# Four small edits to a hybrid attention decode kernel: two weight loads and eight gate halves moved, eight semaphores joined into one, five extra matmuls

## What is computed

```python
def _project_in(x, pos, norm_pre, w_in, ...):
    xn = _rmsnorm(x, norm_pre)
    (qa, kvc, kvs, kvw, gn, ga, qd, kvd, krp, gb, ma, mb) = jnp.split(xn @ w_in, IN_OFFSETS, axis=-1)
...
def _mla_attend(q_lat, q_pe, t, c, kr, pos_k):
    s = (jnp.einsum('bqhc,bsc->bhqs', q_lat, c) + jnp.einsum('bqhr,bsr->bhqs', q_pe, kr)) * MLA_SCALE
    mask = (pos_k[None, :] <= t[:, None])[None, None]
    p = _masked_softmax(s, mask)
    return jnp.einsum('bhqs,bsc->bqhc', p.astype(c.dtype), c)
...
def _merge_out(x, o_a, o_lat, gates, ...):
    pa = (o_a * jax.nn.silu(ga)) @ w_proj_a
    pb = (o_b * jax.nn.silu(gb)) @ w_proj_b
    h = jax.nn.sigmoid(ma) * pa + jax.nn.sigmoid(mb) * pb
    return x + _rmsnorm(h @ w_out, norm_post)
```

## Time and profile before

| | us |
|---|---|
| median of 3 runs | 703.12 |
| all runs | 701.88, 703.12, 706.72 |
| the profiled execution | 701.88 |
| its span, first to last instruction | 700.1 |
| outside of the span | 1.8 |
| PE busy in the span | 666.3 (95%) |
| mean granted clock of TensorE | 0.996 of full |

### The profile page before, as it was taken

One profiled execution on the slowest core, in us unless ns is written; L12 is line 12 of the kernel. 1 busy time (PEld: TensorE's weight loads), 2 busy tenths in 40 slices (PEclk: granted clock), 3 DMA queues, 4 the chain that ended last, 5 costly groups with the idle time before them and its releaser, 6 DMA issues.

```text
span 700.1 us, 15279 instructions
## 1 busy us (share of the span) xinstructions
PE 666.3 (95%) x5767; PEld 439.9 (63%) x5767; DVE 437.8 (63%) x1231; ACT 211.5 (30%) x579; POOL 63.9 (9%) x68
## 2 busy tenths in 40 slices
PE   9999999999999978899999998799999999999996
PEld 4444444644476655667677686578778888885452
DVE  3297899688677757766566565427486656553344
ACT  0402214565344444434444433211101111110211
POOL 0353441031000000220211000000000000000000
PEclk9999999999999999999999999999999999999999
DMA  8999996888899999978858889965411111045010
GB/s 338 414 415 418 419 418 279 308 252 285 315 311 384 386 400 388 401 248 287 304 166 305 310 268 360 391 259 203 158 60 61 61 60 61 1 163 229 30 61 32
DMA packets 66371, 178.65 MB, mean 255 GB/s; under 512 B 7065, under 2 KB 15538, under 8 KB 59258
## 3 DMA queue, kind: packets, MB, share of 16 engines
q1 hardware_dynamic: 55672, 124.88, 49.0%
q0 software_dynamic: 7840, 48.38, 17.3%
q10 hardware_dynamic: 2786, 4.42, 1.8%
HBM read 169.12 MB, written 12.72 MB: 260 GB/s over the span
## 4 chain that ended last, share of the span: by engine, by line
PE 80%; DMA 8%; DVE 5%; SPq 3%; ACT 2%; issue 2%; DVEq 0%; ACTq 0%
PE bank L1420 19%; PE bank L854 12%; PE bank L1460 8%; PE bank L1264 7%; DMA ring<-latent 4%; PE bank L1131 4%; PE bank L1233 4%; PE bank L1248 4%; PE bank L1153 3%; PE bank L1017 3%; PE bank L1139 3%; DMA projP<-x 3%; PE bank L1452 2%; SPq L627 2%; PE bank L1200 2%
## 5 line engine op out<-in xcount | busy, mean ns | idle before, releaser
L854 PE MATMUL bank<-W,XG 128*128 128x494 f32 x192 | 83.6, 580 | 0.9 <-DVE projP L1793 0.9
L2447 DVE TENSOR_TENSOR projP<-projP,bank 128x260 f32<-128x260 f32 x83 | 33.8, 422 | 45.2 <-PE bank L1420 44.4
L1264 PE MATMUL bank<-W 128*128 128x260 f32 x256 | 60.4, 389 | 0.0
L1678 ACT ACTIVATE projP<-bank,projP 128x128 f32<-128x128 f32 (+3 forms) x96 | 49.7, 524 | 30.9 <-DVE projP L2149 30.5
L1481 ACT ACTIVATE projP<-bank 128x128 f32<-128x128 f32 (+5 forms) x87 | 33.9, 391 | 83.0 <-PE bank L1420 47.5
L854 PEld LDWEIGHTS bank<-W,XG 128*128 128x128 f32 x192 | 35.2, 192 | 36.6 <-issue 35.0
L1481 ACT ACTIVATE W<-bank 128x512 f32<-128x512 f32 (+2 forms) x69 | 40.1, 582 | 55.2 <-PE bank L897 13.3
L1264 PEld LDWEIGHTS bank<-W 128*128 128x128 f32 x256 | 47.4, 190 | 11.0 <-issue 4.1
L2149 DVE CUSTOM_DVE_ANT_0 bank<-bank,maskb 128x128 f32<-128x128 f32 (+3 forms) x96 | 45.6, 509 | 7.8 <-PE bank L1131 7.1
L1460 PE MATMUL bank<-ring,W 128*128 128x512 f32 x112 | 49.6, 594 | 0.0
L1131 PE MATMUL bank<-W 64*128 64x128 f32 (+7 forms) x192 | 46.1, 467 | 1.1 <-ACT projP L1678 0.7
(11 more groups left out here) (434 smaller groups left out, 1109.8 us busy)
## 6 DMA issues: line engine op xcount, KB each, us to landing
ring<-latent SPq DMA_DIRECT2D x200, 256.0 KB, 5.1
XG<-latent SPq DMA_DIRECT2D x56, 256.0 KB, 5.4
W<-w_gate SPq DMA_DIRECT2D x12, 1024.0 KB, 6.2
W<-w_attn SPq DMA_DIRECT2D x16, 494.0 KB, 12.4
rope_rows<-ring SPq DMA_DIRECT2D x8, 512.0 KB, 7.3
KRR<-rope_rows ACTq DMA_DIRECT2D x16, 256.0 KB, 5.9
ring<-w_out SPq DMA_DIRECT2D x2, 2048.0 KB, 9.5
o_win<-win SPq DMA_DIRECT2D x1, 4088.0 KB
```

Of the source, the lines that this page charges most:

```text
L854: mm = pe.matmul(bank[2 * (u % 2) + n][:, 0:GW], XG[:, k * TOK + tl * P:k * TOK + (tl + 1) * P], w_part(half, k, n), start=(k == 0), stop= ...
L1264: mm = pe.matmul(bank[6][:, 0:HALF], gate_w[g % 2][:, at:at + P], X2[:, k * TOK + hf * HALF:k * TOK + (hf + 1) * HALF], start=(k == 0), st ...
L1678: act.activation(Pb[u % 4][:, 0:w], bank[u % 2][:, 0:w], ACT.Exp, bias=NMp[:, u:u + 1], scale=-1.0, accum_out=RSp[:, u:u + 1]).then_inc(S[ ...
```

## The change

Four edits:

1. `G_at`: half 6 goes from step 33 to 31, 7 from 34 to 33, 8 from 37 to 34, 9 from 38 to 35, 10 from 41 to 37, 11 from 43 to 38, 12 from 45 to 41, 13 from 47 to 43. Steps 31 and 35 gain a half, steps 45 and 47 lose theirs. The apply steps follow.
2. The second halves of `w_attn` all signal one semaphore, `w_in_rest`, and PE waits once, ahead of unit 4, until all eight have landed.
3. On SP gate(3) goes from behind part 23 to behind part 21, gate(4) from behind part 29 to behind part 24.
4. Ahead of the wait for the latent part of pairs 6, 12, 13, 14 and 15, PE runs one more matmul of 128x512 into bank 5, whose result nobody reads.

```diff
-        G_at = {d: i for i, d in enumerate((23, 25, 26, 27, 29, 30, 33, 34, 37, 38, 41, 43, 45, 47, 48, 49))}
+        G_at = {d: i for i, d in enumerate((23, 25, 26, 27, 29, 30, 31, 33, 34, 35, 37, 38, 41, 43, 48, 49))}
...
             for k in range(KM):
-                sp.dma_start(W[:, (KM + k) * 2 * GW:(KM + k + 1) * 2 * GW], t["w_attn"][:, k, 2 * GW:]).then_inc(S[f"w_in{k}"], 16)
+                sp.dma_start(W[:, (KM + k) * 2 * GW:(KM + k + 1) * 2 * GW], t["w_attn"][:, k, 2 * GW:]).then_inc(S["w_in_rest"], 16)
...
             gate(2)
-            for m in range(19, 24):
+            for m in range(19, 22):
                 latents(m)
             gate(3)
-            for m in range(24, 30):
+            for m in range(22, 25):
                 latents(m)
             gate(4)
+            for m in range(25, 30):
+                latents(m)
...
                 for k in range(KM):
-                    if u == 4:
-                        pe.wait_ge(S[f"w_in{k}"], 32)
+                    if u == 4 and k == 0:
+                        pe.wait_ge(S["w_in_rest"], 16 * KM)
...
                     pe.wait_ge(S["dp"], mla[p2]["q"])
+                if i2 == 0 and p2 in KEPT_BUSY:
+                    pe.matmul(bank[5][:, :], ident, qrT[:, 0:512], start=True, stop=True)
                 job_landed(pe, J_MLA + m)
...
+            KEPT_BUSY = (6, 12, 13, 14, 15)
```

## The result

The change took 711.19 us in the median of 8 runs (708.47 to 713.39), the kernel before 705.90 in the median of 8 (701.88 to 707.75). The ratio is 1.0084 with an interval of 1.0054 to 1.0113: slower by 5.9 us, worked out on 705.9 (the medians differ by 5.3). The profiled execution took 711.43 us, its span is 709.6.

A forecast was written before the change was run, and what follows sets the result against it. PE, busy 666.3 of 700.1 us, was taken to bound the kernel. Unit 4's wait 3.6, extra matmuls 1.1 and step 47's stretch 1.0 sum to 5.7; 701.88 gives 707.6, plus 1.2 to the median: 708.8 us, range 703.5 to 711.5.

The forecast's parts named there:

- the bound between "same" and "slower": Whole kernel: 1% (7.0 us) about marks what a measurement can tell from no change; chance of within 1%: 0.69.
- the clock behind the wait in unit 4: Behind PE's 3.6 us pause ahead of unit 4: no fall of the granted clock; a fall would cost 1.7 us.
- the account of step 47: Step 47: PE waits 5.1 us for part 30 in place of 4.15, the clock falls again; net +1.0 us.
- The wait in unit 4: Ahead of unit 4: PE stands until the eighth w_attn chunk lands, +3.6 us taken whole, bounds 0 and 5.3.
- the fourth rival: Unit 4: the stall is swallowed later by a wait that does not follow PE; 705.2 us, chance 0.10.
- the first rival: Unit 4: the clock also falls behind the wait of 3.6 us; 710.5 us, slower by over 1%, chance 0.21.
- The extra matmuls: 0.89 us each: hidden at steps 19, 43 and 47, 0.17 shows at 45, 0.89 at 41; together +1.1 us.
- Steps 31 and 35: Each gains a gate half of 3.70 us with no idle time to cover it: 7.4 us, lost again at 45 and 47.
- the fifth rival: Steps 31 and 35: the added halves fill time in which PE would have stood; not slower, 701.4 us, chance 0.05.
- The third rival: Part 30 lands no earlier, held up by part 31 behind it, not gate(4) ahead; +2.7, 711.5 us, chance 0.06.
- The second rival: Step 47: the extra matmul keeps PE busy and the clock stays at 1.00; 707.5 us, chance 0.16.

The follow-up runs named there:

- the late-gate run: The kernel before with gate(4) alone put behind part 31 on SP, w_v still ahead of parts 30 and 31: 699.4 us, ratio 0.9909.
- the joined semaphore alone: The kernel before with only the one shared w_attn semaphore and PE's single wait ahead of unit 4: 712.6 us, ratio 1.0105.

## Why the prediction was right or wrong

**The size** was right, in part by luck: +5.7 forecast, +5.9 measured. Of the 6.3 us that the table has without the clock, the wait is 3.8 (3.6 forecast), the extra matmuls at steps 19 to 45 are 2.2 (1.1), steps 31, 35 and 45 to 48 together 0.6 (1.0), and small gains that I did not look for -0.3. The errors in the parts cancel to 0.6. The forecast of 708.8 us is 2.4 below the measured 711.19, inside the range, and that is the base: the median of before moved by 2.8, from 703.12 (3 runs) to 705.90 (8 runs). The forecast set its own profiled execution 1.2 under the median; with eight runs it stands 4.0 under.

**The step that failed**, for the outcome, is the bound between "same" and "slower". I wrote that 1% (7 us) is about what a measurement can tell from no change. With 8 runs on each side the interval is 0.6% wide, and 0.84% is clear of zero. A forecast of +0.8% should have been called slower; most of my chance was put on "within 1%" because of this bound, not because of the mechanism. In the mechanism, the term that failed is the clock behind the wait in unit 4, which I put at nothing and which measured 1.7 us, and the account of step 47; both are taken up below.

**The wait in unit 4** came as forecast: 3.67 us against 3.6, taken whole, since nothing later gave it back (the fourth rival is out). The page "DMA: Bandwidth & Descriptors" of the Trainium skill, section "Why a DMA increments its semaphore by 16 and not by 1", speaks for a semaphore for each slot, so that a count tells which load is complete. No run here shows the page's case; what the runs show is that giving the separate semaphores up cost 1.05% alone.

**The clock behind it** was wrong: I took no fall, because 3.6 was nearer to the 3.2 that kept the clock than to the 4.15 that lost it. It fell, at a price of 1.7 us as rows 10 had said. The mechanism of the first rival (0.21) is what happened, in all three profiles with this wait unfilled. Its time, 710.5, does not follow from it: over the runs the clock of the change is no lower than that of before, so other falls of before's runs have their place here. Which ones, no run shows. Reading a bound from one pause on either side was the error: later profiles show pauses of 2.94 and 3.1 with a fall, and 2.91 and 3.47 without. The Trainium skill, page "TensorE: Matmul & The Clock Gate", section "HAM oscillation — how this bites in real kernels", tells of a kernel in which every DMA wait, of about 3 to 5 us, closes the gate. The trace agrees at unit 4 (3.67 us), but not at the window, where the wait of 3.1 us in the same execution kept the clock; the fall at part 29 came behind 1.99 us, a shorter wait than the page's.

**The extra matmuls** were forecast at +1.1. Step 41 came as said (0.9 against 0.89). Step 19 was not hidden (0.7 net): the 1.41 of the earlier trace rows is the wait for part 13 at step 20, while the extra matmul stands ahead of part 12, where PE has no idle time. I had taken the second group of L1233 for the first. The wait for part 13 can still swallow it one step later: with edit 2 undone it fell from 1.41 to 0.92, in the change only to 1.35. Step 45 cost 0.8 and not 0.17: its wait stayed at 0.64, because the last page of part 28 took 6.19 us to land in place of 5.24. Why it did, no run shows. It is not the extra matmul ahead of it as such: with the extra matmuls alone the wait shrank to 0.15, near the nothing that was forecast, but with only the one of step 47 it was 0.21 as well, so half a us at this wait is within what single profiles differ by. By the ratios all of this is under what could be resolved (1.0014, interval 0.9984 to 1.0045).

**Steps 31 and 35** cost 3.7 each, as forecast; the fifth rival is out.

**Step 47** was wrong in its parts and near in its sum. I forecast one wait of 5.1 for part 30 and a fall of the clock behind it, net +1.0. There were three waits: 1.99 for part 29, which I had not looked at, 0.55 for part 30 and 1.11 for part 31, with the fall behind the first. Steps 45 to 48 came to -6.9, which is +0.5 once the 7.4 of steps 31 and 35 are set against it. What I missed is that the part ahead of the one I looked at comes under pressure as well, since the half of step 45 had given its load the time. The last page of part 30 took 7.9 us to land in the change, near the 7 that I named. The third rival is out by the late-gate run: there it took 5.74, with part 31 behind it as ever. So the order of the loads was worth 3.9 us of landing time, more than the 2.7 that I had worked out from the size of `gate(4)`. The second rival was not put to the test in the change, where the clock held behind part 30 but the pause was only 0.55; with the extra matmul of step 47 alone it fell, behind 2.94.

**What I had not counted**: the fall near 149, which is not of the change. A fall between 141 and 157 stands in 11 of the 13 profiles here and not in that of before.

## What to carry to other kernels

Give each load its own semaphore where work comes chunk by chunk: one wait for the sum puts the last landing ahead of the first use, and the clock may fall behind it. When a load is late, first look at what stands ahead of it on its queue and is needed later: moving 1,024 KB behind took 0.9% off, while moving compute away from the same steps only made room for waits. Before a result is called "no change", work out what the interval of the planned runs will be, and before a profiled execution is used as a base, see where it stands among the runs.

## What the runs showed of the hardware

The clock does not follow the length of a pause alone. At step 47 it held behind 2.91 us and fell behind 2.94, at the window it held behind 3.47 in one profile and fell behind 2.96 in another, and in the change it fell behind 1.99. One minus the clock, summed over a fall, was 1.7 us for every fall in the profiles of before and of the change (the one at the end of the span left out), and 3.4 for longer ones in other kernels: with the joined semaphore alone all three (67 to 75, 149 to 157, 460 to 468) were of that length. A second place of falls is near 141 to 149 (11 of 13 profiles), in a stretch of small matmuls whose pauses are 0.8 us at most in each of the 13.

The scatter of the runs of one kernel goes with it. In the 73 runs of before, the mean granted clock of a run lies around 0.990 and its time around 705.2, and the two are correlated at -0.84: longer runs are runs with more time at 1.2 GHz. The profiled execution of before, at 0.996 and with a single fall, was at the fast end.
